# An encoder's feed forward stage: the sum with x stays in its PSUM bank, and ScalarE makes x, its high part and its square

## What is computed

```python
for l in range(DEPTH):                                   # DEPTH = 2
    x = x + 0.5 * swiglu(rmsnorm(x, ffn1_norm[l]), ...)  # (silu(h @ w_gate) * (h @ w_up)) @ w_down
    h = rmsnorm(x, mix_norm[l])
    u = h @ w_in[l]
    y = concatenate([rmsnorm(conformer_conv(u[..., :c0], ...)),
                     rmsnorm(windowed_gqa_sink(u[..., c0:c1], ...))])
    x = x + y @ w_out[l]
    x = x + 0.5 * swiglu(rmsnorm(x, ffn2_norm[l]), ...)
return rmsnorm(x, final_norm)
```

## Time and profile before

| | |
|---|---|
| median of 3 runs | 1998.28 us (1997.71 to 1998.99) |
| the profiled execution | 2000.01 us, its span 1998.2 us |
| granted TensorE clock, mean | 0.957 |
| TensorE matmuls | 1864.7 us busy, 93% of the span |
| VectorE | 1131.7 us, 57% |
| ScalarE | 749.0 us, 37% |
| GpSimd | 1184.9 us, 59% |
| DMA | 83 GB/s |

### The profile page before, as it was taken

One profiled execution on the slowest core, in us unless ns is written; L12 is line 12 of the kernel. 1 busy time (PEld: TensorE's weight loads), 2 busy tenths in 40 slices (PEclk: granted clock), 3 DMA queues, 4 the chain that ended last, 5 costly groups with the idle time before them and its releaser, 6 DMA issues.

```text
span 1998.2 us, 25193 instructions
## 1 busy us (share of the span) xinstructions
PE 1864.7 (93%) x8132; PEld 1524.7 (76%) x8132; DVE 1131.7 (57%) x1221; ACT 749.0 (37%) x968; POOL 1184.9 (59%) x591
## 2 busy tenths in 40 slices
PE   6999999985888999999999999999758989999996
PEld 5888888764676888888878888887647768888885
DVE  7554443499967645443364544336988775444434
ACT  3433322332764433322333333223246543333221
POOL 4544467675757544457754445777657664444674
PEclk8999999987898999999999999999868989999998
DMA  4322233311002222223322222332110123222331
GB/s 147 115 96 94 83 87 95 116 53 64 1 32 74 95 98 98 95 72 93 119 98 94 96 103 71 95 108 103 41 39 1 64 70 109 94 94 82 86 97 60
DMA packets 53425, 166.68 MB, mean 83 GB/s; under 512 B 6000, under 2 KB 6256, under 8 KB 53360
## 3 DMA queue, kind: packets, MB, share of 16 engines
q1 hardware_dynamic: 52128, 163.78, 25.7%
q10 hardware_dynamic: 1232, 2.10, 0.3%
HBM read 163.76 MB, written 2.10 MB: 83 GB/s over the span
## 4 chain that ended last, share of the span: by engine, by line
PE 80%; DVE 10%; issue 8%; ACT 1%; POOL 0%; DVEq 0%; DMA 0%; ACTq 0%; POOLq 0%
PE bank L1092 26%; PE bank L1093 25%; PE bank L1094 25%; DVE xs_lo L723 2%; DVE odd_taps L864 1%; PE bank L1210 1%; DVE y_conv L864 1%; DVE xs_hi L791 1%; PE bank L1197 1%; DVE work L750 1%; DVE q_lo L876 1%; DVE prob L1019 1%; PE bank L1110 0%; PE bank L1199 0%; POOL pool_taps L420 0%
## 5 line engine op out<-in xcount | busy, mean ns | idle before, releaser
L369 POOL TENSOR_TENSOR w_lo<-stage,w_hi 128x1024 fp32r<-128x1024 f32 x352 | 907.2, 2579 | 645.6 <-ACT w_hi L498 645.2
L1092 PE MATMUL bank<-xs_hi,w_hi 128*128 128x512 f32 x1688 | 672.6, 398 | 33.3 <-DVE xs_lo L723 21.7
L498 ACT ACTIVATE w_hi<-stage 128x1024 fp32r<-128x1024 f32 x352 | 372.1, 1059 | 883.8 <-PE bank L1094 880.1
L1093 PE MATMUL bank<-xs_lo,w_hi 128*128 128x512 f32 x1688 | 666.6, 395 | 0.0
L1094 PE MATMUL bank<-xs_hi,w_lo 128*128 128x512 f32 x1688 | 665.7, 394 | 0.0
L1092 PEld LDWEIGHTS bank<-xs_hi,w_hi 128*128 128x128 f32 x1688 | 322.6, 191 | 108.4 <-DVE xs_lo L723 27.8
L750 DVE TENSOR_TENSOR work<-bank,rstd 128x512 f32<-128x512 f32 x220 | 150.1, 688 | 401.1 <-PE bank L1094 400.1
L1094 PEld LDWEIGHTS bank<-xs_hi,w_lo 128*128 128x128 f32 x1688 | 322.7, 191 | 68.5
L1093 PEld LDWEIGHTS bank<-xs_lo,w_hi 128*128 128x128 f32 x1688 | 323.1, 191 | 67.6 <-issue 1.4
L1092 PE MATMUL bank<-h_hi,w_hi 128*128 128x512 f32 x704 | 273.9, 389 | 0.0
L1093 PE MATMUL bank<-h_lo,w_hi 128*128 128x512 f32 x704 | 273.9, 389 | 0.0
(11 more groups left out here) (152 smaller groups left out, 1541.6 us busy)
## 6 DMA issues: line engine op xcount, KB each, us to landing
stage<-w_gu SPq DMA_DIRECT2D x176, 512.0 KB, 3.3
stage<-w_down SPq DMA_DIRECT2D x64, 384.0 KB, 3.2
stage<-w_down SPq DMA_DIRECT2D x64, 320.0 KB, 2.9
stage<-w_in SPq DMA_DIRECT2D x24, 512.0 KB, 3.2
stage<-w_out SPq DMA_DIRECT2D x16, 512.0 KB, 3.2
x<-xT ACTq DMA_DIRECT2D x4, 512.0 KB, 6.6
stage<-w_in SPq DMA_DIRECT2D x8, 256.0 KB, 2.5
out<-result SPq DMA_DIRECT2D x8, 256.0 KB, 2.2
```

Of the source, the lines that this page charges most:

```text
L369: nc.gpsimd.tensor_tensor(w_lo[:, r, :], stage[:, r, :], w_hi[:, r, :].bitcast(F32), ALU.subtract).then_inc(split, 1)
L498: nc.scalar.activation(w_hi[:, r, :], stage[:, r, :], ACT.Copy).then_inc(hi_made, 1)
L1092: nc.tensor.matmul(to, wh, mh, start=first, stop=False)
L1093: nc.tensor.matmul(to, wh, ml, start=False, stop=False)
```

## The change

After the sum the tile stays in its bank. VectorE writes `0.5 * bank + x` back into the bank (`x_summed`). ScalarE, which now has a loop written out over m, makes from the bank the new x in SBUF (`x_kept`) and the high part (`x_hi_made`), and from the new x the square (`squared`). VectorE then makes the low part out of the bank. In ScalarE's order the first three slots of the next tile stand ahead of the wait for the sum, the fourth behind the square; in the last tile of the second feed forward no slots are made, as before, but the three activations and their wait stand there. The down tiles no longer count as turns in `evicted` (FFN_TURNS), so TensorE waits for a bank's low part: before tile m of 4 and up for that of tile m - 4, and before the first tile of every stage that takes x for the fifth low part (`BANKS + 1`). The loops over the down tiles are written out on ScalarE, VectorE and TensorE. GpSimd's and SyncE's code is the same.

```diff
-FFN_TURNS, MIX_TURNS = 2 * NF + ND, 32
+FFN_TURNS, MIX_TURNS = 2 * NF, 32

 # ScalarE
-            def ffn_steps(l, base, turns, name, last):
+            def ffn_steps(l, base, turns, name, last, next_prep, gain_at):
...
-                def down(m):
-                    for j in range(4):
-                        high(l, at + m * 4 + RING + j, j, uses_of(l, at // RING + 1 + m, 0))
-
-                with act.Fori(0, ND - 1) as m:
-                    down(m)
-                if not last:
-                    down(ND - 1)
+                for m in range(ND):
+                    later = not (last and m == ND - 1)
+                    if later:
+                        for j in range(3):
+                            high(l, at + m * 4 + RING + j, j, uses_of(l, at // RING + 1 + m, 0))
+
+                    act.wait_ge(x_summed, (2 * l + int(last)) * ND + m + 1)
+                    nc.scalar.activation(x[:, m, :], bank[m % BANKS][:], ACT.Copy).then_inc(x_kept, 1)
+                    nc.scalar.activation(xs_hi[:, m, :], bank[m % BANKS][:], ACT.Copy,
+                                         scale=par[:, gain_at + m:gain_at + m + 1]).then_inc(x_hi_made, 1)
+                    act.wait_ge(x_kept, (2 * l + int(last)) * ND + m + 1)
+                    act.wait_ge(sq_added, next_prep * ND + m)
+                    nc.scalar.activation(sq[:], x[:, m, :], ACT.Square).then_inc(squared, 1)
+                    if later:
+                        high(l, at + m * 4 + RING + 3, 3, uses_of(l, at // RING + 1 + m, 0))

 # VectorE
-                with dve.Fori(0, ND // 4) as i:
-                    dve.wait_ge(par_landed, l * 16 + 16)
-                    for j in range(4):
-                        m = i * 4 + j
-
-                        tile_summed(l, base + 2 * NF + m * 4 + 3)
-                        nc.vector.scalar_tensor_tensor(chunk(x, m), bank[j][:], 0.5, chunk(x, m), ALU.mult,
-                                                       ALU.add).then_inc(evicted, 1)
-                        own(l, turns + 2 * NF + m)
-                        dve.wait_ge(sq_added, prep * ND + m)
-                        nc.vector.tensor_tensor(sq[:], chunk(x, m), chunk(x, m), ALU.mult).then_inc(squared, 1)
-                        high_x(m, par, gain_at)
-                        split_x(prep, m, par, gain_at)
+                dve.wait_ge(par_landed, l * 16 + 16)
+                for m in range(ND):
+                    tile_summed(l, base + 2 * NF + m * 4 + 3)
+                    nc.vector.scalar_tensor_tensor(bank[m % BANKS][:], bank[m % BANKS][:], 0.5, x[:, m, :], ALU.mult,
+                                                   ALU.add).then_inc(x_summed, 1)
+
+                    dve.wait_ge(x_hi_made, prep * ND + m + 1)
+                    nc.vector.scalar_tensor_tensor(xs_lo[:, m, :], bank[m % BANKS][:],
+                                                   par[:, gain_at + m:gain_at + m + 1],
+                                                   xs_hi[:, m, :].bitcast(F32), ALU.mult,
+                                                   ALU.subtract).then_inc(x_split, 1)

 # TensorE, model_tile
                 if first == 0:
                     open_bank(l, turn)
+                    if prep is not None:
+                        pe.wait_ge(x_split, prep * ND + BANKS + 1)

 # TensorE, ffn_steps
-                with pe.Fori(0, ND // 4) as i:
-                    for j in range(4):
-                        turn = turns + 2 * NF + i * 4 + j
-                        open_bank(l, turn)
+                for m in range(ND):
+                    if m < BANKS:
+                        open_bank(l, turns + 2 * NF + m)
+                    else:
+                        pe.wait_ge(x_split, next_prep * ND + m - BANKS + 1)
...
```

More of the change, by code:

```diff
@@ L215, in encoder @@
         x_made = sem("x_made")
+        x_summed = sem("x_summed")
+        x_kept = sem("x_kept")
         x_half = sem("x_half")
@@ L540, in _ @@
                     high(l, j, j, uses_of(l, 0, 0))
-                ffn_steps(l, 0, 0, "ffn1", last=False)
+                ffn_steps(l, 0, 0, "ffn1", False, prep_no(l, 1), G_MIX)
                 def mix_high(s):
@@ L695, in _ @@
                         mix_high(20 + m // 2)
-                ffn_steps(l, FFN_SLOTS + MIX_SLOTS, FFN_TURNS + MIX_TURNS, "ffn2", last=True)
+                ffn_steps(l, FFN_SLOTS + MIX_SLOTS, FFN_TURNS + MIX_TURNS, "ffn2", True, prep_no(l, 3), G_NEXT)
             root(DEPTH, "ffn1", by_token=True)
@@ L1149, in model_tile, with ffn_steps @@
                         between[k]()
-            def ffn_steps(l, base, turns, h_base, prep, name):
+            def ffn_steps(l, base, turns, h_base, prep, name, next_prep):
                 for j in range(4):
@@ L1157, in ffn_steps @@
                         model_tile(l, base + i * 4 + j, j, turns + i * 4 + j, j)
-                with pe.Fori(0, ND // 4) as i:
-                    for j in range(4):
-                        turn = turns + 2 * NF + i * 4 + j
-                        open_bank(l, turn)
[L1162 to L1170, removed]
+                for m in range(ND):
[3 more added lines that the diff above has]
+                        pe.wait_ge(x_split, next_prep * ND + m - BANKS + 1)
+                    f = 0
+                    for n, count in enumerate(DOWN):
+                        take(l, base + 2 * NF + m * 4 + n)
+                        pe.wait_ge(h_split, l * 2 * NF + h_base + f + count)
+                        for k in range(count):
+                            last = triple(bank[m % BANKS][:], *weights(n, k), h_hi[:, f, :], h_lo[:, f, :], f == 0,
+                                          f == NF - 1)
+                            f += 1
+                        last.then_inc(used, 1)
             pe.wait_ge(consts_v, 1)
@@ L1174, in _ @@
             with pe.Fori(0, DEPTH) as l:
-                ffn_steps(l, 0, 0, 0, prep_no(l, 0), "ffn1")
+                ffn_steps(l, 0, 0, 0, prep_no(l, 0), "ffn1", prep_no(l, 1))
                 def in_tile(t, between=None):
@@ L1314, in _ @@
                           {(0, 1): conv_statistic})
-                ffn_steps(l, FFN_SLOTS + MIX_SLOTS, FFN_TURNS + MIX_TURNS, NF, prep_no(l, 2), "ffn2")
+                ffn_steps(l, FFN_SLOTS + MIX_SLOTS, FFN_TURNS + MIX_TURNS, NF, prep_no(l, 2), "ffn2", prep_no(l, 3))
             pe.wait_ge(sq_added, (DEPTH * 3 + 1) * ND)
```

## The result

The changed kernel takes 2009.44 us in the median of 6 executions (2004.02 to 2013.41), the kernel before 1998.52 us (1997.71 to 2004.21): the ratio, taken over all executions, is 1.0049, with a 95% interval of 1.0028 to 1.0071 (the two medians alone give 1.0055). In nine more executions it took 2005.94 us (2004.25 to 2013.86), with the same ratio, 1.0049 (1.0033 to 1.0066), where the medians alone give 1.0039. The change makes the kernel about 0.5% slower. One thing is needed to read the single numbers: the executions of most kernels here fall into two groups 6 to 8 us apart, which the traces of the changed kernel put down to how long TensorE's clock stays at half in the mixer's attention, and the profiled execution of the changed kernel (2013.41 us, span 2011.6) is one of the upper group, that of the kernel before (2000.01) one of the lower.

What follows compares the result with a forecast made beforehand. TensorE was taken as the bound, carrying 80% of the chain of waits. Terms 3.4+10.3-4.0+0+0.4 = +10.1 us, made in the profiled execution and carried to the 1998.28 median, gave 2008.4 us, 0.5% slower; range 2001.5 to 2014.

Steps and rivals of the forecast that it cites:

- Inside the stage 0: Within the down-projection tiles: unrolling, moving work to ScalarE and relieving VectorE gain 0, hidden by 15 us of matmuls.
- The chain on ScalarE: After T, the stage's last matmul's end: x copied by T+1.50, high part T+2.2, square T+2.8, low part T+3.0 to T+3.8.
- Feed forward to mixer, +3.4: Two joints: statistic 0.95 us later each, plus one clock fall of 1.5 us; +3.4 us (1.4 to 6.8).
- Layer 0 to layer 1, +10.3: One joint: next layer's first splits queue behind the last sum's wait, square, branch and table load; +10.3 us (6.6 to 11.0).
- Mixer to second feed forward, -4.0: Two joints: waiting for the fifth low part keeps early chunks in one piece; -4.0 us (-4.8 to +1.0).
- the best case: Mixer to second feed forward: second tile starts at 642.8 at full clock, 2.2 us ahead by 646.36.
- Start 0, end +0.4: Kernel start: first tile held until 18.91, 0 us (to +1.9); kernel end: reciprocal later, +0.4 us (0 to 0.8).
- The branch and the table load: Rival, layer 0 to layer 1: ScalarE's branch and load covered, joint +6.7, total 2002.1 us; chance 0.13.
- The clock came back after each joint: Rival denied here: TensorE's clock stays down at mixer and second feed forward joints, 2017.5 us; chance 0.13.
- TensorE's unrolled turns: Rival, down projection: each loop turn hid a 1.85 us stall, so unrolling gives back 7.4 us, 2001.0 us; chance 0.02.
- the fourth slot starved no tile: Rival denied here: late fourth-slot low weights cost 1 us in each of 28 tiles, 2036 us; chance 0.01.

Runs made afterwards that it cites:

- the second set: The changed kernel run again, unaltered, in nine more executions against the kernel before: 2005.94 us, ratio 1.0049.
- Experiments 1 and 2: First: changed kernel without the fifth-low-part wait in the second feed forward, 2011.09 us; second: kernel before with only that wait added there, 1993.32 us.

## Why the prediction was right, point by point

The forecast was 2008.4 us and 0.5% slower; measured were 2009.44 and 2005.94, both by a ratio of 1.0049 to the kernel before beside them. The order of the terms and their signs hold.

- **Inside the stage 0**: right. 14.96 us a tile on both sides.
- **The chain on ScalarE**: copy 0.60 (taken 0.58), high part 0.68 (0.69), square 0.63 (0.62), sum in the bank 0.70 (0.69), low part 0.75 (0.74 to 1.57). Two of the durations overlap by 0.1 us at each hand-over on the engine, so that the square is done at T+2.46, as I had allowed for with 2.6 and not taken.
- **Feed forward to mixer, +3.4**: the mechanism was right, the size was off. ScalarE's high half began at T+2.36, not T+2.8, because of those overlaps, and the statistic stands at T+7.15, not T+7.7, so the two joints cost 0.45 and 0.39 us instead of 0.95 each. The fall of the clock that I priced at 1.5 us did not come: TensorE idled 1.71 us, not 2.1, and the granted clock is 1.00 on both sides of it. Measured +0.84. The wait that went was 1.19 us in the kernel before; I had taken 1.0 from another joint.
- **Layer 0 to layer 1, +10.3**: +10.24, and +10.09 in the second set. TensorE went on at T+9.40 for T+9.6, the second tile started at T+17.02 for T+17.0. The row's 0.02 us between a table load and the next activation was there again (1003.22 + 1.28 to 1004.52). The Trainium skill, "ScalarE: Activation LUTs", section "What ACT_TABLE_LOAD costs", adds a drain of 1.38 us to each switch to another table set; this trace does not show it.
- **Mixer to second feed forward, -4.0**: -4.25, in both executions. Experiments 1 and 2 show from both sides that the added wait is its cause. The clock was back 5.1 us after the fifth part, just within the 5.2 us that I had given it, and the second tile started 8.46 us after that part, where the best case said 8.4, at full clock.
- **Start 0, end +0.4**: -0.03 and +0.42 (VectorE's reciprocal at T+6.06, before T+5.64).
- **The sum of the joints** was therefore 7.25 us by the first trace and not 10.1. What carried the first median to 10.9 is the attention, which the prediction took as unchanged: it had no term for a stretch whose time differs from one execution to the next by up to 6.7 us with the same code, though the far end of its range came from just such a clock. That the first median lies 1 us from the forecast is thus partly luck: two errors, the mixer joints 2.6 us too dear and the attention left out, have opposite signs. The second median, 2005.94, is close to what the joints alone give (1998.28 and 7.0 to 7.3 is 2005.3 to 2005.6).
- **The rivals.** The branch and the table load were not covered: 1.81 us of issue and 1.28 us of load stand in ScalarE's timeline behind the square. The clock came back after each joint. TensorE's unrolled turns gave nothing back (14.96 us a tile on both sides), and the fourth slot starved no tile.

## What to carry to other kernels

When a wait is put on an engine that also feeds others, list what is queued behind it at the last turn of the loop, where the next stage's first work stands: here the second tile of the next layer started 17.0 us behind T instead of 6.75, because of weights that ScalarE had been free to split 10 us ahead of T. Relieving an engine that waits for the bound engine anyway (9.21 us idle per tile became 12.26) gains nothing; only the joints count. And where a chain of producers delivers a piece every few microseconds to an engine whose clock falls in the gaps, it can pay to hold that engine back until the rest can be done without a gap.

## What the runs showed of the hardware

TensorE's granted clock in the attention differs between executions of one kernel. Windows of 20 us of the attention of layer 1, us of busy time of TensorE, its weight loads, VectorE, ScalarE and GpSimd, then the granted clock; first the profiled execution of the changed kernel, then that of its second set:

```profile
1475.00:1495.00 20.00, 15.92 (x69) 12.15 (x69) 16.05 (x34) 8.05 (x24) 7.37 (x7) 0.78 0.16 54
1495.00:1515.00 20.00, 18.48 (x57) 13.74 (x57) 18.22 (x41) 13.27 (x35) 15.40 (x17) 0.56 0.00 1
1515.00:1535.00 20.00, 20.00 (x60) 15.29 (x60) 14.38 (x32) 10.36 (x25) 10.87 (x13) 0.50 0.00 1
1535.00:1555.00 20.00, 20.00 (x109) 16.22 (x108) 15.88 (x35) 12.66 (x33) 14.00 (x15) 0.92 0.01 1
```

```profile
1475.00:1495.00 20.00, 16.71 (x74) 12.81 (x75) 16.20 (x40) 8.40 (x25) 6.27 (x7) 0.84 0.09 28
1495.00:1515.00 20.00, 20.00 (x60) 15.02 (x61) 18.09 (x40) 14.61 (x38) 16.70 (x18) 0.50 0.01 2
1515.00:1535.00 20.00, 19.26 (x91) 14.84 (x90) 15.47 (x34) 12.73 (x32) 11.61 (x14) 0.82 0.00 0
1535.00:1555.00 20.00, 17.04 (x96) 13.76 (x95) 18.94 (x44) 14.06 (x38) 16.86 (x19) 1.00 0.00 1
```

At a granted 0.50 TensorE is busy all 20 us with 60 matmuls, where it does 96 to 109 at 1.00 and 0.92: the lower level makes it the bound of a part where it otherwise has gaps. In steps of 4 us, the stay at half lasts from about 1495 to 1520 in the second and from about 1498 to 1536 in the first, some 25 and some 38 us, and layer 1's mixer with its attention takes 244.56 against 251.30 us. The mean clocks of all executions go the same way: 0.957 to 0.959 in the changed kernel's lower group and 0.951 to 0.954 in its upper one; in the kernel before, where 78 executions have a clock on record, 0.955 to 0.960 below 2003 us and 0.950 to 0.953 above. What sets its length here was not found. The change is not needed for it, since the kernel before has such executions too, though none of them was traced.

After 1.71 us of idling (386 to 392 us) the granted clock was still 1.00; the statistic's 1.12 us instead of 1.02 is the same 0.1 us that the first matmul behind a wait takes longer at full clock, 0.50 for 0.39. TensorE was at half after 5.44 and 9.40 us, for 5.1 and 4.4 us of unbroken work.
